# Two loops over registers written out: the scan's groups and the expert pairs that every input has

## What is computed

```python
u = rms_norm(h, norm_mix);  h = h + ssd_mixer(u, ...)
u = rms_norm(h, norm_ffn);  h = h + hier_moe(u, ...)

# ssd_mixer: 8 groups of 4 heads (head 64, state 128), 8 chunks of 128 tokens
zxbcdt = u @ w_in;  xbc = silu(causal_dwconv(xbc, conv_w, conv_b))
y = y_diag + y_off + xs * d_skip          # chunked scan, states carried from chunk to chunk
yg = rms_norm(y * silu(z) by group);  return yg @ w_out

# hier_moe: top-1 of 4 expert groups, then top-2 of its 8 experts; 32 experts, hidden width 512
order = argsort(expert_id)                # rows sorted by expert, padded to blocks of 128
hid = silu(xb @ w_gate[e]) * (xb @ w_up[e]);  y_rows = hid @ w_down[e]
y[row_token] += y_rows * row_weight
```

## Time and profile before

| | before |
|---|---|
| median of 3 runs | 1627.29 us (1625.89 to 1629.35) |
| profiled execution | 1625.55 us |
| its span, first to last instruction | 1623.7 us |
| PE busy | 1560.9 us, 96% of the span |
| DVE, ACT, POOL busy | 78%, 44%, 38% |
| scan phase | from 0 to about 990 us |
| expert phase | from about 1000 us to the end |
| granted TensorE clock, mean | 0.991 |

### The profile page before, as it was taken

How to read it: one execution, slowest core, us unless ns; L and a number is a source line. 1 busy time by engine, 2 the same in 40 slices (tenths; PEclk the granted TensorE clock), 3 DMA queues, 4 the chain that set the end, 5 groups by cost and what they waited for, 6 DMA issues and landing times. The chain is left out here.

```text
span 1623.7 us, 26207 instructions
## 1 busy us (share of the span) xinstructions
PE 1560.9 (96%) x7488; PEld 1258.7 (78%) x7488; DVE 1273.9 (78%) x2317; ACT 717.4 (44%) x1231; POOL 621.5 (38%) x749
## 2 busy tenths in 40 slices
PE   6999999999999999999999987999999999999996
PEld 5778888878888788888888876777777777777774
DVE  6668868768778778688687788989778888788884
ACT  5333232233232233332322444755666665666662
POOL 2232131131131221311311313376666666666564
PEclk9999999999999999999999998999999999999998
DMA  4132121221121221221312474999999999999992
GB/s 159 40 82 53 50 81 33 59 73 35 52 72 46 60 72 31 68 59 46 84 34 72 167 239 167 398 359 366 371 367 375 373 379 360 377 377 376 384 348 67
DMA packets 142995, 292.75 MB, mean 180 GB/s; under 512 B 21596, under 2 KB 72204, under 8 KB 142896
## 3 DMA queue, kind: packets, MB, share of 16 engines
q1 hardware_dynamic: 127904, 266.29, 46.6%
q0 software_dynamic: 14992, 25.22, 4.3%
HBM read 291.81 MB, written 25.30 MB: 195 GB/s over the span
## 5 line engine op out<-in xcount | busy, mean ns | idle before, releaser
L2080 DVE TENSOR_TENSOR gu_lo<-w_gu,gu_hi 128x1024 fp32r<-128x1024 f32 x256 | 306.3, 1223 | 48.1 <-ACT gu_hi L1912 32.7
L1333 PE MATMUL proj<-uTh,wl 128*128 128x512 f32 x768 | 308.7, 402 | 6.8 <-issue 4.1
L1335 PE MATMUL proj<-uTh,wh 128*128 128x512 f32 x768 | 301.1, 392 | 0.0
L1334 PE MATMUL proj<-uTl,wh 128*128 128x512 f32 x768 | 300.0, 391 | 0.0
L1912 ACT ACTIVATE gu_hi<-w_gu 128x1024 fp32r<-128x1024 f32 x256 | 260.9, 1054 | 56.9 <-PE g_ps L1985 33.9
L558 POOL TENSOR_TENSOR wl<-raw,wh 128x512 fp32r<-128x512 f32 x96 | 129.5, 1366 | 385.0 <-ACT wh L654 385.0
L1333 PEld LDWEIGHTS proj<-uTh,wl 128*128 128x128 f32 x768 | 144.9, 189 | 37.4 <-issue 7.0
L707 ACT ACTIVATE xbc<-v 128x512 f32<-128x512 f32 x64 | 40.5, 633 | 292.2 <-DVE v L1052 292.2
L1335 PEld LDWEIGHTS proj<-uTh,wh 128*128 128x128 f32 x768 | 144.7, 188 | 31.9
L1334 PEld LDWEIGHTS proj<-uTl,wh 128*128 128x128 f32 x768 | 145.2, 189 | 28.7
L1052 DVE SCALAR_TENSOR_TENSOR v<-xr,cw,v 128x512 f32<-128x512 f32 x192 | 146.2, 761 | 14.7 <-DVE v L1052 0.5
(11 more groups left out here) (316 smaller groups left out, 3301.0 us busy)
## 6 DMA issues: line engine op xcount, KB each, us to landing
w_gu<-in_moe_w_gate_dram SPq DMA_DIRECT2D x128, 512.0 KB
w_gu<-in_moe_w_up_dram SPq DMA_DIRECT2D x128, 512.0 KB
w_d<-in_moe_w_down_dram SPq DMA_DIRECT2D x128, 512.0 KB
raw<-in_ssd_w_in_dram SPq DMA_DIRECT2D x96, 256.0 KB, 3.5
E<-acum_dram SPq DMA_DIRECT2D x64, 256.0 KB, 3.4
raw<-in_ssd_w_out_dram SPq DMA_DIRECT2D x28, 256.0 KB, 2.9
hacc<-in_x_dram SPq DMA_DIRECT2D x8, 512.0 KB, 7.5
out_dram<-hacc SPq DMA_DIRECT2D x8, 512.0 KB, 4.7
```

Of the source, the lines that this page charges most:

```text
L1333: nc.tensor.matmul(out, al, bh, start=start, stop=False)
L1334: nc.tensor.matmul(out, ah, bl, start=False, stop=False)
L1335: return nc.tensor.matmul(out, ah, bh, start=False, stop=stop)
L2080: vec.tensor_tensor(wl[:, j % RING, :], weights.gate_up(b, j), wh[:, j % RING, :].bitcast(F32), ALU.subtract).then_inc(w_lo, 1)
```

## The change

Three edits:

- groups: all eight groups are written out with constant numbers; no loop is left in the scan phase.
- pairs: 14 pairs are written out in place of 3. The Fori then runs from pair 14 to the bound, and the last pair follows as before. For these inputs the Fori runs once (pair 14) and pair 15 is the last.
- npairs: each engine reads entry 0 (k = 1) or entry 1 (k = 15); DVE writes two entries in place of four.

```diff
         def groups(eng, body):
 
-            with eng.Fori(0, (GROUPS - 2) // 2) as i:
-                body((i, 0))
-                body((i, 1))
-            body((None, LASTG - 1))
-            body((None, LASTG))
+            for g in range(GROUPS):
+                body((None, g))
...
-        def pairs(eng, body, peeled=3):
+        def pairs(eng, body, peeled=NE // 2 - 2):
 
             def less(k):
 
-                return eng.value_load(npairs[0:1, k - 1:k], min_val=NE // 2 - k, max_val=NE // 2 + 8 - k)
+                n = 0 if k == 1 else 1
+                return eng.value_load(npairs[0:1, n:n + 1], min_val=NE // 2 - k, max_val=NE // 2 + 8 - k)
...
-                for k in range(4):
-                    link(vec.tensor_scalar(npairs[:, k:k + 1], few[:, 8:9], float(NE // 2 - 1 - k), None, ALU.add))
+                for n, k in enumerate((1, NE // 2 - 1)):
+                    link(vec.tensor_scalar(npairs[:, n:n + 1], few[:, 8:9], float(NE // 2 - k), None, ALU.add))
```

## The result

| | before | changed |
|---|---|---|
| median | 1627.29 us (5 runs, 1622.65 to 1629.35) | 1613.45 us (5 runs, 1611.94 to 1615.53) |
| profiled execution, span | 1625.55 us, 1623.7 us | 1612.88 us, 1610.5 us |

The changed kernel is faster: ratio 0.9921, 95% interval 0.9902 to 0.9940. A second set of 6 runs gave 1613.75 us (experiment 13).

What follows compares the result with a forecast made beforehand. PE was taken to bound the kernel, with DMA close behind in the expert phase. Savings of 6.1 + 1.6 + 0.4 = 8.1 us from the median of 1627.29 gave 1619.2 us, range 1614.5 to 1624.0.

Steps and rivals of the forecast that it cites:

- Jumps of the scan loop: Scan phase, PE: two jumps back cost 3.92 and 2.17 us; writing the loop out saves 6.1 us.
- Register work: Scan: six groups lose register instructions, 0.27 us each, saving 1.6 us; bounds nothing and 3.6 us.
- npairs: Expert phase, DVE: two operations fewer on the path PE waits for, saving 0.4 us.
- Pair loop: Expert phase: eleven jumps and the register work go, costed at nothing because queued work and split weights cover them.
- Rival (A): Expert phase: 16 more code packets come late under full DMA, costing 33 us, time 1652; chance 0.07.
- (B): Scan: the stall belongs to the place, not the jump; only 1.6 + 0.4 + 0.2 us go, time 1625.1; chance 0.10.
- (C): Expert phase also gets smoother as POOL and DVE reach yb sooner: 2.3 us more, time 1616.9; chance 0.12.
- The sum: Whole kernel: 6.1 + 1.6 + 0.4 = 8.1 us saved, 7.7 us of it in the scan, giving 1619.2 us.
- The range: Whole kernel: 1614.5 to 1624.0 us for 8 in 10, allowing the register work's upper bound and the median's scatter.

Runs made afterwards that it cites:

- experiment 13: The changed kernel run once more, unchanged: 1613.75 us.
- 1: The kernel before with only the scan groups written out, pair loop and npairs as before: 1616.07 us, ratio 0.9927.
- 3: The kernel before with the scan loop's three trips as three loops of one trip each: 1615.65 us, ratio 0.9922.
- 6: The kernel before with its scan loop kept and a branch prefetch hint added on every engine: 1623.10 us, ratio 0.9982.
- 5: The kernel before with the scan written out on PE alone, the other four engines keeping their loop: 1621.07 us, ratio 0.9974.
- 9: The kernel before with 14 pairs written out on POOL alone, scan loop and four npairs entries kept: 1625.25 us, ratio 0.9998.
- 10: The kernel before with the pairs written out on all engines but POOL, scan loop and four npairs entries kept: 1624.55 us, ratio 0.9990.
- 4: The kernel before with the scan written out on every engine but PE, which keeps its loop: 1624.14 us, ratio 0.9982.
- 2: The kernel before with only fourteen pairs written out and two npairs entries, scan loop as before: 1625.26 us, ratio 0.9985.
- 12: The changed kernel with the overflow-table work and npairs moved from pairs 0 to 2 into pairs 3 to 8: 1613.09 us, ratio 0.9917.
- 14: The kernel before with only the scan groups written out, run once more beside the changed kernel: 1612.35 us, ratio 0.9920.
- 7: The kernel before with six pairs in the pair loop's body and two trips: 1638.05 us, ratio 1.0074.

## Why the prediction missed, step by step

- **Jumps of the scan loop, -6.1.** The mechanism was right: 1 and 3 take the gain with the jumps gone, 6 shows that the jump waits for code. The size was right too, 2 x 3.17 = 6.3 us by the mean of seven profiles, but with luck: the prediction read one profile, in which the clock fell behind one jump of two, as it does in the mean. It took the 3.92 and 2.17 us as the prices of a first and a second jump; they are the prices with and without a clock fall, and how many falls a run has changes. Nor did it see that DVE stalls at the same time (5), so that PE's jump alone was not the thing to remove.
- **Register work, -1.6: the step that failed.** What the written-out scan gives beside the jumps is 9.6 - 6.3 = 3.3 us by the means. Groups 1, 3 and 5 differ by 0.40, 0.33 and 0.56 us, group 0 by 0.96, groups 2 and 4 behind their first chunk by 1.0 together. Some 0.8 us of this are two long waits for sq with a fall of the clock behind them, in kernels 9 and 10, so 2.5 to 3.3 us stand where 1.6 stood. The step took one group of one profile, 0.27 us, whose difference was among the smallest, and times six. The mechanism (ACT's sq comes late) and the upper bound of 3.6 held. It is not PE's work (4), but that of the other engines.
- **npairs, -0.4.** The wait went from 1.09 to 0.70 us, as worked out. Pairs 0 to 2 take 111.3 us in the mean with two entries (changed, 2, 13) and 112.1 with four (the others without 12), these between 111.3 and 113.3; whether anything of it reaches the end stays open (12).
- **Pair loop, 0.** Nothing here contradicts it but kernel 2, which had 2.1 us by medians, with an interval that excludes zero; kernels 9, 10, 13 and 14 don't bear it out. What is left, between nothing and some 2 us, is not settled.
- **Rival (A)** is false here: 14 packets were fetched under a DMA share of 1.00 and PE waited for none. **(B)** is false by the changed kernel and 3. **(C)** is not borne out: 9 and 10 can't be told from before, 14 is not slower than 13, and pairs 3 to 14 differ by 0.7 us where it asked for 2.3.
- **The sum.** The scan's part by the mean of the profiles is 683.6 - 674.0 = 9.6 us where 7.7 stood. The spans of the six looped profiles (without 7) have a mean of 1623.5, those of the five with a written scan (changed, 1, 3, 13, 14) 1613.2: 10.3 us. So the scan's part was undersized by 1.9 us, nearly all of it in the register term. The other part of the miss is the base: the median of 1627.29 us, from three runs at first, is 1.2 over the mean of before's four medians, 1626.1. By these and the two medians of the changed kernel the change is worth 1626.1 - 1613.6 = 12.5 us. By the medians of the kernels whose spans are compared, 1625.2 for the six and 1614.3 for the five, it is 10.9 us. The 1.6 us between the two are not traced to a place; kernels that should be alike lie as far apart (1612.35 to 1616.07 us with the scan written out).
- **The range** let the register term reach 3.6 us and gave the jumps no room at all, though a row showed one of them with a slower matmul behind it and the other without.

## What to carry to other kernels

Before costing a loop's jump, count the instructions of its body on each engine. Here the short bodies jumped in 0.2 to 0.3 us, the long ones waited 2.9 to 5.5 us, and the limits lay between 309 and 369 records on ACT and between 1,054 and 2,104 on PE. The engines' stalls hide one another, so write out the loop on every engine that stalls, or shorten its body for all. Put no long-bodied loop where PE and DMA are both full: there a single jump cost 12 us. A stall's price has two values if the clock may fall behind it, so take it from several profiles, and take a small difference between groups from several groups.

## What was not expected of the hardware

- Behind 7 of 14 jumps with 1.4 to 2.6 us of idle PE the granted clock was 0.50 for 3.4 us, behind the other 7 it stayed at 1.00, and the length of the gap doesn't tell which. With the hint there was neither a gap nor a fall at the jumps.
- The hint shortened PE's jump from 4.2 to 0.69 us, while groups without a jump grew by 0.1 to 1.6 us; ACT stood for 2.0 us behind the loop's end.
- One jump of a body of six pairs under full DMA: 4.2 us on PE's sequencer and 5.2 to 5.5 on the others, 1.7 us of idle PE, 12.0 us of the median.
- 14 code packets for PE among 47,000 of a full DMA load came without any wait that the view shows, where a jump over a long body left 1.4 to 2.6 us of idle PE.
